# Three more row buffers for the expert gathers of the second layer's context mixer, paid for with half of the Gram buffer

## The chip, the cores and the metric

One core of a Trainium2 chip runs the whole program. The metric is the device time in microseconds (us), as the median of several executions.

## What is computed

The program is a two-layer block over 256 tokens and 256 context tokens (width 1024), followed by one hybrid layer. Only the first block touches the change. In each of its layers:

```
hc = modulate(xc, ...);  yc, ctx_states = token_mixer(hc, emit = not last)   # context
h  = modulate(x, ...);   y, _ = token_mixer(h, states = ctx_states)          # tokens
x  = x + gt1 * y
x  = x + gt2 * peer(modulate(x, ...))                                        # experts of the tokens
if not last: the same for xc
```

`token_mixer` holds a recurrence over tokens for 16 heads and two directions (`rwkv_scan`), here in chunks of 64 tokens. In the second layer the context mixer has `emit=False`: it only makes the states. `peer` picks for every token 8 x 16 experts out of 16384, and

```
u = take(peer_u, eidx);  act = gelu(einsum('td,thkd->thk', h, u)) * gw
v = take(peer_v, eidx);  out = einsum('thk,thkd->td', act, v)
```

so each token needs 128 rows of `peer_u` and 128 rows of `peer_v`, 4 KB each.

## The kernel before

**The job.** Since `peer` of one stream doesn't depend on the mixer that comes next, its work is spread through the stages of that mixer. `k.job` is the running job. It has 256 rows to take: row `r` is one indirect DMA (512 KB: for each of 128 tokens its expert's row of `peer_u`), issued by GpSimd in `gather_row`, and one VectorE instruction over 128 x 1024 in `use_rows` (L2092), which makes 128 dot products. When the first 128 rows are done, `weigh_tile` makes weights of them, and from then on values are open: a batch is four gathers of `peer_v` (`gather_part`, L2149), a small copy (`pick_weights`) and 8 matmuls of 512 columns (`use_batches`, L2118).

**Buffers and order.** Row gathers use the slots in `job.shared.slots`, four of them here, in turn (`job.turn % len(slots)`). Row `r` goes into the slot that row `r-4` had, so its gather waits until VectorE has used row `r-4`. Batches use eight other slots, four in the weight ring and four in `more`, so two batches are in the air. The program of every stage is written out ahead: VectorE's part says after which of its own steps it takes how many rows, TensorE's part when it takes a batch, and then `fetch_rows` writes GpSimd's part for the stage: all rows and batches that the stage uses and does not have yet, and the ones that fit in the slots after that. It sorts them by the step at which their slot came free. GpSimd works through this list in order, so a gather that waits holds up all behind it.

**The stage in question.** `rwkv` of the second layer's context mixer, with `k.job` the tokens' job of the first layer. `project_keys` comes first (18 weight blocks, 26 rows), then eight calls of `rwkv_unit` (four quarters of the heads, two directions). I call them units 0 to 7. A unit, with the names that the rows show:

1. VectorE makes `KR` (L911), takes 4 rows, makes `Ld`, `LdT`, `NT` (L923, L924) from TensorE's products (L962, L963), takes 1 row, makes `X` (L991).
2. `invert_pairs`: 12 steps in which TensorE multiplies (L724, L719) and ScalarE copies each product back (L700). VectorE isn't in this chain when a job runs; beside it, it takes 18 rows (14 when values are open) and makes `G` (L1002), the masked Gram products, after steps 4 and 5. After step 8 TensorE and ScalarE make the sigmoids of the next unit (L780, L781).
3. The recurrence: TensorE and ScalarE pass `R`, `W`, `S`, `state` to and fro (L1121 to L1154, L1044 to L1067), once for each of two chunks. Meanwhile VectorE makes the sums of the next unit (L790 to L801) and its rates (L823 to L825) and takes 3 rows. Between the two chunks ScalarE raises the sums to exponentials (L809, L811), from which VectorE makes `C` (L846).
4. All engines meet before the next unit's `KR`.

Units 0 to 3 run with values closed and take 26 rows each. Before unit 4 the tile is weighed; units 4 to 7 take 22 rows and, in all, about five batches each. The rest of the job is done in `finish_experts`, where eight row slots are in use and the matrix engine waits for the rows.

`G` has 128 columns per product, of which the mixer without `emit` uses 64. Its flat form also serves as `squares` in `project_keys`, ahead of the units.

Of the kernel before, what the change touches and what calls it, by code (L numbers as in the profile page):

```python
# [13 lines left out]
P = 128  # L14
# [22 lines left out]
class Core:  # L37


    def __init__(self, nc, ctx):  # L40
# [26 lines left out]
        self.spare_slots, self.own_slots, self.windows = [], False, []  # L67
# [1117 lines left out]
def project_keys(k, L, w, order, rhs, b, first, emit, then=None, mod=None):  # L1185
# [10 lines left out]
    squares = b.G[:].rearrange("p h i n t -> p (h i n t)").rearrange("p (j t) -> p j t", j=8)  # L1196
# [184 lines left out]
def rwkv(k, L, z, states, emit, w, rhs, order, o=None, spare=None, then=None, hosts=None, restore=(), mod=None):  # L1381
# [4 lines left out]
    with ExitStack() as mem:  # L1386
# [4 lines left out]
        with ExitStack() as inner:  # L1391
            u = buffers(k, inner, tot=[2, 2, 4], pc=[2, 2, 4], KR=[2, 2, 256], C=[2, 4, 2, 64], CT=[4, 2, P], G=[2, 2, 4, P], W=[4, 2, 2, 64],
# [11 lines left out]
            units[0].first = True  # L1404
            if hosts is None and k.job is not None:
                more = buffers(k, inner, more=[4, 1024]).more
                hosts = spare_rows(k, 8, *(more[:, j, :] for j in range(4)))
            project_keys(k, L, w, order, rhs, u, units[0], emit, None if emit else then, mod)
            enter_ring(k, hosts)
# [574 lines left out]
class Slot:  # L1984

    def __init__(self, rows, landed):
        self.rows, self.landed = rows, landed
        self.freed, self.taken, self.left, self.step = None, False, 0, 0  # L1990
# [8 lines left out]
    def leave(self, sem, value, step, order=0):  # L1999
        self.freed, self.taken, self.step, self.left = (sem, value), False, step, order  # L2000
# [10 lines left out]
class Experts:  # L2011
# [3 lines left out]
    def __init__(self, shared, lists, x, layer):  # L2015
        self.shared, self.lists, self.x, self.layer = shared, lists, x, layer
        self.row, self.fetched, self.places, self.turn, self.stage = 0, 0, {}, 0, 0
# [62 lines left out]
def use_rows(k, dve, n):  # L2080


    job = k.job
# [3 lines left out]
    for r in range(job.row, min(job.row + n, 2 * SLOTS)):  # L2087
        tile, slot = divmod(r, SLOTS)
        place = place_row(job, r)
# [38 lines left out]
def gather_row(k, pool, r):  # L2128

    job, b = k.job, k.job.shared  # L2130
    place = place_row(job, r)
# [42 lines left out]
def fetch_rows(k, pool):  # L2174
# [5 lines left out]
    rows = range(job.fetched, min(job.row + len(job.shared.slots), 2 * SLOTS))  # L2180
# [3 lines left out]
    wanted, picked = [(place_row(job, r).step, 2, r, 0) for r in rows], 0  # L2184
# [13 lines left out]
def enter_ring(k, more):  # L2198
# [296 lines left out]
def finish_experts(k, job, then=None):  # L2495
# [14 lines left out]
    with ExitStack() as inner:  # L2510
# [3 lines left out]
        b.slots, job.turn = [*own, *extra[0:4]], 4  # L2514
# [67 lines left out]
def choose_last(k, l, dram, x, mod, job, then):  # L2582
# [13 lines left out]
    with ExitStack() as mem:  # L2596
# [11 lines left out]
        b.slots, job.turn = [*own, *extra[8:12]], 0  # L2608
# [1301 lines left out]
```

## Time and profile before

| | us |
|---|---|
| median of 3 runs | 5279.18 |
| lowest, highest | 5279.08, 5311.7 |
| the profiled execution's own time | 5297.07 |
| its span, first to last instruction | 5295.1 |

Busy over the span: TensorE 3740.9 us (71%), VectorE 2454.9 (46%), GpSimd 1706.1 (32%), ScalarE 1087.5 (21%). These shares are means over stages with different limits, so the stage has to be read by itself: units 0 to 7 lie between 2170 and 2723 us of the span. The profiled execution is 17.9 us above the median; durations below come from it.

### The profile page before, as it was taken

How to read it: one execution, taken by the hardware profiler on the slowest of the kernel's cores; microseconds unless marked ns; L12 is line 12 of the kernel's file. 1: busy time of each engine (PE TensorE's matmuls, PEld its weight loads, DVE VectorE, ACT ScalarE, POOL GpSimd, SP SyncE). 2: the span in 40 equal slices, each digit the busy share in tenths (PEclk: the TensorE clock that was granted, in tenths of full speed). 3: DMA queues.
4: the chain of work that ended last, by engine and by line, in shares of the span. 5: the costliest groups of instructions: out<-in, count | busy, mean ns of one | idle time of the engine just before them, and what ended most of it. 6: DMA issues, size and time to landing. Idle time of an engine off the chain costs nothing. (4 is left out here: it accounts for less than half of the span.)

```text
span 5295.1 us, 87998 instructions
## 1 busy us (share of the span) xinstructions
PE 3740.9 (71%) x36238; PEld 2819.0 (53%) x36238; DVE 2454.9 (46%) x5650; ACT 1087.5 (21%) x2789; POOL 1706.1 (32%) x1745
## 2 busy tenths in 40 slices
PE   7989896976767886765645599988430325877788
PEld 6777684864545563654421187776300001766677
DVE  2756547675553264774450023663968240143310
ACT  1234311232222111342310022442100000111300
POOL 0000003245564244465566500000567776000000
PEclk9999997987787897886767799998765667888899
DMA  5423246777786587677789743003799999312242
GB/s 210 132 94 130 89 151 260 263 239 253 270 273 237 213 333 289 228 251 256 271 318 368 301 140 115 3 3 108 287 360 350 362 362 345 124 59 62 88 142 105
DMA packets 298909, 1117.72 MB, mean 211 GB/s; under 512 B 33681, under 2 KB 39073, under 8 KB 289953
## 3 DMA queue, kind: packets, MB, share of 16 engines
q0 software_dynamic: 221184, 805.40, 42.5%
q1 hardware_dynamic: 77344, 306.90, 16.9%
q8 instruction: 280, 4.59, 0.4%
q14 instruction: 101, 0.82, 0.0%
HBM read 1111.13 MB, written 1.05 MB: 210 GB/s over the span
## 5 line engine op out<-in xcount | busy, mean ns | idle before, releaser
L2135 POOL DMA_INDIRECT ring<-in_peer_u,expert_number x624 | 720.4, 1154 | 1204.8 <-DVE expert_number L2446 566.4
L2092 DVE CUSTOM_DVE_ANT_0 ring<-ring,tok 128x1024 f32<-128x1024 f32 x624 | 754.8, 1225 | 482.7 <-DMA ring<-in_peer_u,expert_number 454.8
L2118 PE MATMUL psum<-spare,picked 128*32 128x512 f32 x1472 | 283.2, 870 | 520.5 <-issue 241.5
L2118 PEld LDWEIGHTS psum<-spare,picked 128*32 128x32 f32 x1472 | 60.2, 138 | 737.0 <-issue 736.6
L2149 POOL DMA_INDIRECT spare<-in_peer_v,expert_turned x368 | 352.3, 957 | 157.1 <-issue 92.9
L177 PE MATMUL psum<-h,weight_ring 128*128 128x256 f32 x1728 | 386.0, 387 | 22.6 <-PEq L96 22.6
L177 PEld LDWEIGHTS psum<-h,weight_ring 128*128 128x128 f32 x1728 | 336.3, 195 | 71.7 <-issue 23.9
L1823 PE MATMUL psum<-h,weight_ring 128*128 128x256 f32 x1344 | 294.3, 380 | 3.5 <-PEq L96 3.5
L1823 PEld LDWEIGHTS psum<-h,weight_ring 128*128 128x128 f32 x1344 | 254.8, 190 | 41.7 <-issue 7.5
L1339 PE MATMUL psum<-h,weight_ring 128*128 128x256 f32 x1056 | 236.8, 386 | 8.6 <-PEq L96 8.6
L2149 POOL DMA_INDIRECT weight_ring<-in_peer_v,expert_turned x174 | 181.9, 1045 | 139.0 <-PE psum L2118 90.1
L1339 PEld LDWEIGHTS psum<-h,weight_ring 128*128 128x128 f32 x1056 | 203.3, 194 | 41.3 <-issue 12.7
L2291 DVE SCALAR_TENSOR_TENSOR x_tokens<-psum,gate,x_tokens 128x128 f32<-128x128 f32 x32 | 8.6, 343 | 438.7 <-PE psum L2280 438.7
L2092 DVE CUSTOM_DVE_ANT_0 spare<-spare,tok 128x1024 f32<-128x1024 f32 x144 | 176.0, 1225 | 32.1 <-DMA spare<-in_peer_u,expert_number 24.8
L2118 PE MATMUL psum<-weight_ring,picked 128*32 128x512 f32 x696 | 141.1, 789 | 64.4 <-POOL picked L2169 30.3
L700 ACT ACTIVATE E<-psum 128x256 f32<-128x256 f32 x240 | 90.1, 383 | 419.3 <-PE psum L724 378.0
L2135 POOL DMA_INDIRECT spare<-in_peer_u,expert_number x144 | 160.2, 1113 | 49.6 <-issue 41.3
L2149 POOL DMA_INDIRECT more<-in_peer_v,expert_turned x120 | 119.9, 999 | 138.9 <-PE psum L2118 75.9
L2826 POOL MEMSET picked<- 128x1512 f32 x1 | 1.4, 1358 | 485.5 <-POOLq L96 485.5
L724 PE MATMUL psum<-TT,E 64*64 64x64 f32 x3072 | 125.7, 226 | 43.2 <-ACT TT L700 19.2
L724 PEld LDWEIGHTS psum<-TT,E 64*64 64x64 f32 x3072 | 113.3, 139 | 64.3 <-ACT TT L700 21.4
L1672 DVE SCALAR_TENSOR_TENSOR zc<-u,vec,zc 128x256 f32<-128x256 f32 x336 | 134.7, 482 | 0.0
(617 smaller groups left out, 7368.3 us busy)
## 6 DMA issues: line engine op xcount, KB each, us to landing
weight_ring<-in_w_in SPq DMA_DIRECT2D x226, 512.0 KB
ring<-in_ada_w SPq DMA_DIRECT2D x24, 1024.0 KB, 12.0
weight_ring<-in_w_q SPq DMA_DIRECT2D x48, 512.0 KB
weight_ring<-in_ada_w SPq DMA_DIRECT2D x16, 1024.0 KB, 6.5
weight_ring<-in_w_out SPq DMA_DIRECT2D x32, 512.0 KB
gate_ring<-in_w_gate SPq DMA_DIRECT2D x32, 512.0 KB, 3.6
weight_ring<-in_w_mlp_in SPq DMA_DIRECT2D x32, 512.0 KB
weight_ring<-in_w_mlp_out SPq DMA_DIRECT2D x8, 2048.0 KB
```

Source lines behind the costliest of these rows:

```text
L177: mm = pe.matmul(k.bank(slot, tokens), ring[:, slot, j * P:j * P + P], rhs(j), start=(j == 0), stop=(j == w.kt - 1))
L700: act.activation(out[:, g], product(q, g), ACT.Copy).then_inc(k.act_step.up(), 1)
L724: mm = pe.matmul(product(q, g)[h, n, :], left[h, g, n, :], rhs, start=not onto, stop=True, skip_group_check=onto)
L1339: mm = pe.matmul(k.bank(4 + slot, 256), k.ring[:, slot, j * P:j * P + P], rhs(j), start=(j == 0), stop=(j == 7))
L1672: ins = dve.scalar_tensor_tensor(conv[:, j, :], src, scale, conv[:, j, :], ALU.mult, ALU.add)
L1823: mm = pe.matmul(k.bank(slot, 256), k.ring[:, slot, j * P:j * P + P], normed[:, j, :] if i >= blocks else rhs(j), start=(j == 0), stop=(j ...
L2092: dve.tensor_tensor_reduce(place.rows, place.rows, b.tok[:, tile, :], 1.0, 0.0, ALU.mult, ALU.add, b.dots[:, tile, slot:slot + 1]).then_in ...
L2118: mm = pe.matmul(out, place.window.columns[:, strip, first:first + STRIP], part.rows[:, 512 * half:512 * half + 512], start=(m % BATCHES = ...
L2135: pool.indirect_dma_start(place.rows, None, b.tables["u"], bass.IndirectOffsetOnAxis(ap=b.number[:, r:r + 1], axis=0)).then_inc(place.sem, 16)
L2149: pool.indirect_dma_start(part.rows, None, b.tables["v"], bass.IndirectOffsetOnAxis(ap=job.lists.turned[:, token:token + 1], axis=0)).then ...
L2291: dve.scalar_tensor_tensor(part, k.psum[:, P * j:P * j + P], job.lists.gate[:, j:j + 1], part, ALU.mult, ALU.add).then_inc(k.vec_step.up(), 1)
L2826: pool.memset(lent.picked[:], 0.0).then_inc(k.pool_step.up(), 1)
```

## The change

- In the mixer without `emit` and with a job running, `G` gets 64 columns per product instead of 128 (4 KB per partition given up).
- `more` grows from four rows to seven. The first four serve the batches as before. The other three are row slots, in `k.more_rows`, from the first unit to the end of the last; two of them serve as `squares` before that.
- A row no longer takes the slots in turn. It takes the slot that has been free longest, out of the shared ones and `k.more_rows`. `fetch_rows` gathers ahead as long as a slot is free: seven rows instead of four in the units.
- In the last unit `k.more_rows` is emptied before GpSimd's list is written, so four rows are ahead at its end, as before.

No instruction is added or taken away, other than waits on slots.

```diff
-        G=[2, 2, 4, P]
+        G=[2, 2, 4, P if emit or k.job is None else 64]
...
+            row_hosts = []
+            u.squares = u.G[:]... if emit or k.job is None else None
             if hosts is None and k.job is not None:
-                more = buffers(k, inner, more=[4, 1024]).more
+                more = buffers(k, inner, more=[7, 1024]).more
                 hosts = spare_rows(k, 8, *(more[:, j, :] for j in range(4)))
+                row_hosts = spare_rows(k, 12, *(more[:, j, :] for j in range(4, 7)))
+                u.squares = more[:, 4:6, :]...
             project_keys(k, L, w, order, rhs, u, units[0], emit, None if emit else then, mod)
-            enter_ring(k, hosts)
+            enter_ring(k, hosts, row_hosts)
...
     def leave(self, sem, value, step, order=0):
-        self.freed, self.taken, self.step, self.left = (sem, value), False, step, order
+        self.freed, self.taken, self.step, self.left, self.since = (sem, value), False, step, order, next(Slot.uses)
...
+def row_slots(k, r):
+    slots = [*k.job.shared.slots, *k.more_rows]
+    return [slot for slot in slots if not slot.taken]
+
-def place_row(job, r):
+def place_row(k, r):
+    job = k.job
     if r not in job.places:
-        slots = job.shared.slots
-        job.places[r] = slots[job.turn % len(slots)].take()
-        job.turn += 1
+        job.places[r] = min(row_slots(k, r), key=lambda slot: slot.since).take()
...
-    rows = range(job.fetched, min(job.row + len(job.shared.slots), 2 * SLOTS))
+    rows = range(job.fetched, job.row)
+    while len(rows) + job.fetched < 2 * SLOTS and row_slots(k, job.fetched + len(rows)):
+        rows = range(job.fetched, job.fetched + len(rows) + 1)
+        place_row(k, rows[-1])
...
-        k.spare_slots = [*k.job.shared.weight_ring, *more]
+        k.spare_slots, k.more_rows = [*k.job.shared.weight_ring, *more], rows
...
-        k.spare_slots = []
+        k.spare_slots, k.more_rows = [], []
```

## Rows read from the trace of the kernel before

**Rows 1.** Busy time by stage: units 0, 3 and 6, then a stretch of `finish_experts`

```profile
core 0: us, PE busy (x) PEld busy (x) DVE busy (x) ACT busy (x) POOL busy (x), PEclk, DMA share, GB/s
2170.50:2227.50 57.00, 40.50 (x720) 34.23 (x721) 43.25 (x77) 21.61 (x61) 33.43 (x28) 0.77 0.73 242
...
2337.80:2392.40 54.60, 37.50 (x688) 31.49 (x688) 43.33 (x77) 20.82 (x59) 34.85 (x27) 0.84 0.77 251
...
2568.98:2647.84 78.86, 53.60 (x800) 38.99 (x800) 38.63 (x70) 22.08 (x61) 46.94 (x47) 0.78 0.80 278
...
2738.00:2766.00 28.00, 0.00 (x0) 0.00 (x0) 24.62 (x40) 0.00 (x0) 21.91 (x21) 0.50 0.99 377
```

**Rows 2.** Waits of VectorE, units 0 to 3 (us in total, times, longest)

```profile
DVE ring L2092 <- DMA ring<-in_peer_u,expert_number: 42.2, 54, 2.0
```

**Rows 3.** VectorE in order of time: unit 0, then `finish_experts` (start, us)

```profile
2174.33 1.22 DVE L2092 CUSTOM_DVE_ANT_0 ring<-ring,tok 128x1024 f32<-128x1024 f32 x1 [0.80 <-DMA ring<-in_peer_u,expert_number]
2177.24 1.22 DVE L2092 CUSTOM_DVE_ANT_0 ring<-ring,tok 128x1024 f32<-128x1024 f32 x1 [1.68 <-DMA ring<-in_peer_u,expert_number]
...
2180.88 1.23 DVE L2092 CUSTOM_DVE_ANT_0 ring<-ring,tok 128x1024 f32<-128x1024 f32 x1 [0.41 <-DMA ring<-in_peer_u,expert_number]
...
2196.47 1.23 DVE L2092 CUSTOM_DVE_ANT_0 ring<-ring,tok 128x1024 f32<-128x1024 f32 x1 [0.67 <-DMA ring<-in_peer_u,expert_number]
...
2205.05 1.22 DVE L2092 CUSTOM_DVE_ANT_0 ring<-ring,tok 128x1024 f32<-128x1024 f32 x1 [0.85 <-DMA ring<-in_peer_u,expert_number]
...
2738.04 1.23 DVE L2092 CUSTOM_DVE_ANT_0 ring<-ring,tok 128x1024 f32<-128x1024 f32 x1
...
2770.39 1.23 DVE L2092 CUSTOM_DVE_ANT_0 spare<-spare,tok 128x1024 f32<-128x1024 f32 x1 [0.57 <-DMA spare<-in_peer_u,expert_number]
```

**Rows 4.** ScalarE in order of time, ends of units 0 to 3

```profile
2218.23 0.63 ACT L809 ACTIVATE E<-E 128x512 f32<-128x512 f32 x1 [0.47 <-DVE E L796]
...
2273.06 0.63 ACT L809 ACTIVATE E<-E 128x512 f32<-128x512 f32 x1 [3.00 <-DVE E L801]
...
2328.54 0.63 ACT L809 ACTIVATE E<-E 128x512 f32<-128x512 f32 x1 [4.26 <-DVE E L796]
...
2377.64 1.28 ACT L809 ACT_TABLE_LOAD   x1
2383.61 0.63 ACT L809 ACTIVATE E<-E 128x512 f32<-128x512 f32 x1 [4.69 <-DVE E L801]
...
2387.72 0.94 ACT L1067 ACTIVATE state<-psum,pc 128x64 f32<-128x64 f32 x4 [0.77 <-PE psum L1154]
```

**Rows 5.** VectorE in order of time, end of unit 3

```profile
2391.62 0.69 DVE L846 TENSOR_TENSOR C<-X,E 64x512 f32<-64x512 f32 x1
```

**Rows 6.** GpSimd and TensorE in order of time, unit 1

```profile
2263.39 1.12 POOL L2135 DMA_INDIRECT ring<-in_peer_u,expert_number  x1 [0.30 <-issue]
...
2266.09 1.27 PE L1154 MATMUL psum<-W,CT 128*64 128x64 f32 x16 [0.88 <-issue]
...
2268.40 0.69 PE L1121 MATMUL psum<-S,KR 64*64 64x64 f32 x8 [1.04 <-issue]
```

**Rows 7.** TensorE (busy, clock, DMA share, GB/s) by stretches, units 1 and 6

```profile
2240.00:2258.00 18.00, 14.53 (x326) 1.00 0.85 282
...
2572.00:2575.00 3.00, 2.81 (x65) 1.00 0.93 317
...
2578.00:2581.00 3.00, 1.83 (x10) 0.50 0.97 365
2581.00:2584.00 3.00, 1.17 (x6) 0.50 1.01 392
```

**Rows 8.** TensorE in order of time, unit 5, under 8 gathers

```profile
2524.08 1.12 PE L724 MATMUL psum<-constants,X 64*64 64x64 f32 x16 [3.74 <-issue]
2528.42 1.12 PE L724 MATMUL psum<-X,NT 64*64 64x64 f32 x16 [3.23 <-issue]
```

**Rows 9.** Waits of VectorE from 2400 to 2715 us, units 4 to 7

```profile
DVE ring L2092 <- DMA ring<-in_peer_u,expert_number: 114.3, 38, 9.9
```

More of the change, by code:

```diff
@@ L1 @@
+import itertools
 import math
@@ L1195, in project_keys @@
     kz = z[:, 8:16, :]
-    squares = b.G[:].rearrange("p h i n t -> p (h i n t)").rearrange("p (j t) -> p j t", j=8)
+    squares = b.squares
     norm = b.TT[0:16].rearrange("p i n t -> p (i n t)")[:, 0:256]
@@ L1391, in rwkv @@
         with ExitStack() as inner:
[L1392 removed]
+            u = buffers(k, inner, tot=[2, 2, 4], pc=[2, 2, 4], KR=[2, 2, 256], C=[2, 4, 2, 64], CT=[4, 2, P], G=[2, 2, 4, P if emit or k.job is None else 64], W=[4, 2, 2, 64],
                         R=[2, 2, 64], S=[2, 2, 64], LdT=[2, 4, 64], NT=[2, 4, 64], Ld=[2, 4, 64], E1=[2, 4, 64], E2=[2, 4, 64],
@@ L1404, in rwkv @@
             units[0].first = True
+            row_hosts = []
+            u.squares = u.G[:].rearrange("p h i n t -> p (h i n t)").rearrange("p (j t) -> p j t", j=8) if emit or k.job is None else None
             if hosts is None and k.job is not None:
-                more = buffers(k, inner, more=[4, 1024]).more
+                more = buffers(k, inner, more=[7, 1024]).more
                 hosts = spare_rows(k, 8, *(more[:, j, :] for j in range(4)))
+                row_hosts = spare_rows(k, 12, *(more[:, j, :] for j in range(4, 7)))
+                u.squares = more[:, 4:6, :].rearrange("p n c -> p (n c)").rearrange("p (j t) -> p j t", j=8)
             project_keys(k, L, w, order, rhs, u, units[0], emit, None if emit else then, mod)
-            enter_ring(k, hosts)
+            enter_ring(k, hosts, row_hosts)
             for n, operands in enumerate(units):
@@ L1984 @@
 class Slot:
+    uses = itertools.count(1)
     def __init__(self, rows, landed):
         self.rows, self.landed = rows, landed
-        self.freed, self.taken, self.left, self.step = None, False, 0, 0
+        self.freed, self.taken, self.left, self.step, self.since = None, False, 0, 0, 0
     def take(self):
@@ L2016, in __init__ @@
         self.shared, self.lists, self.x, self.layer = shared, lists, x, layer
-        self.row, self.fetched, self.places, self.turn, self.stage = 0, 0, {}, 0, 0
+        self.row, self.fetched, self.places, self.stage = 0, 0, {}, 0
         self.batch, self.batches_fetched, self.groups = 0, 0, {}
@@ L2183, in fetch_rows @@
     batches = range(first, max(last, min(last + ahead, job.open_batches())))
-    wanted, picked = [(place_row(job, r).step, 2, r, 0) for r in rows], 0
+    wanted, picked = [(place_row(k, r).step, 2, r, 0) for r in rows], 0
     for m in batches:
@@ L2195, in fetch_rows, with enter_ring @@
             gather_row(k, pool, n)
-def enter_ring(k, more):
+def enter_ring(k, more, rows):
     if k.job is not None:
-        k.spare_slots = [*k.job.shared.weight_ring, *more]
+        k.spare_slots, k.more_rows = [*k.job.shared.weight_ring, *more], rows
 def leave_slots(k, pe):
@@ L2513, in finish_experts @@
         extra = spare_rows(k, 8, *(spare.spare[:, j, :] for j in range(20)))
-        b.slots, job.turn = [*own, *extra[0:4]], 4
+        b.slots = [*own, *extra[0:4]]
         k.spare_slots, k.own_slots, k.windows = extra[4:20], True, [Window(spare.picked[:, n]) for n in range(6)]
@@ L2607, in choose_last @@
         own, windows, marks = b.slots, k.windows, {}
-        b.slots, job.turn = [*own, *extra[8:12]], 0
+        b.slots = [*own, *extra[8:12]]
         k.spare_slots, k.own_slots, k.windows = [*extra[12:16], *extra[0:8], *b.weight_ring], True, [Window(lent.picked[:, n]) for n in range(6)]
```

6 lines of the change are left out of this document (3 added, 3 removed).

## The prediction

> **What bounds the kernel now.** The page of the whole span can't decide this: VectorE is busy for 46% of it, and the change acts on 8 of its stages. I read first the busy time of each stage, then the waits of VectorE in the stages with the new slots, then the order of time at the end of a unit, to see whether a wait of VectorE delays anything.
>
> In units 0 and 3 VectorE is busy for 43.3 of 57.0 and 54.6 us, TensorE for 40.5 and 37.5 [rows 1]; units 1 and 2, 54.9 and 55.4 us long, repeat the pattern. VectorE waits there for one thing that matters: a row that has not landed, 42.2 us in 54 waits over the four units [rows 2], some 10.5 in each. So 43.3 of work, 10.5 of waits and under 1 us of meeting the others fill the unit: VectorE has no other idle time, and it is the engine that ends it. The reader should see this at the end of unit 3 too. ScalarE has loaded its table by 2378.9 us and then waits 4.69 us for VectorE's sums [rows 4]. `C` ends at 2392.3 [rows 5], after `state` at 2388.7 [rows 4]. Both say that TensorE and ScalarE were ready earlier.
>
> Why do rows come late? In the long stretch beside the inversion four rows take from 2196.47 to 2205.05, 2.15 us each, with a wait for the landing before nearly every one [rows 3]. VectorE alone would do one in 1.15 us, the step from one row to the next where none is late. With four slots one row costs a quarter of the loop "use, gather, land, use". In `finish_experts`, with eight slots, 23 steps from 2738.04 to 2770.39 take 32.35 us, 1.41 us each [rows 3], and there the DMA engines are at a share of 0.99 with 377 GB/s [rows 1]. So with four slots the loop sets the pace, and with eight the DMA engines do.
>
> **The change part by part.**
>
> *Narrower `G`, moved `squares`.* The same instructions on the same counts of elements, in other places. The squares lie in two of the new rows, which hold no row before the first unit. I take 0; no row bounds a difference in placement, and I allow 1 us either way for the 32 writes of `G` in the eight units together.
>
> *Slots by longest free instead of in turn.* With one ring of slots that all go through the same hands this is the same order. Where slots are added (the finishing stages) the fresh ones come first, as before. In the last choice of experts the fresh ones now come ahead of the old ones, and none of these has anything to wait for. 0 us.
>
> *Seven slots in units 0 to 3.* The first three gathers of unit 0 need no used slot. From then on row `r` waits for `r-7`. A unit needs 26 rows: at 1.41 us each that is 36.7 us of supply against 43.3 us of VectorE's own work, so the supply is enough on the mean. Within the unit the hard stretch is 18 rows beside the inversion, 18 x 1.15 + 2 x 0.67 for `G` = 22 us, against 18 x 1.41 = 25.4 us less what is ahead. Seven slots hold up to 9.9 us of supply, of which some 5 rows are there when the stretch begins (5 rows were taken just before it). That covers the 3.4 us that are missing. I leave 1 us of waits per unit, 4 in all, and remove 38 of the 42 us from VectorE.
>
> *What is late next.* With its waits gone VectorE is no longer last. From the order of time: the exponentials could start earlier by the wait that ScalarE shows, 0.47, 3.00, 4.26 and 4.69 us in units 0 to 3 [rows 4], together 12.4 us. `state` then ends 3.65 us ahead of where `C` ended (2392.31 less 2388.66 in unit 3 [rows 4, 5]; the same difference in the other three), 14.6 us over four units. In unit 0, the two waits ahead of `Ld`, 0.80 and 1.68 us, and 0.41 us after it delay the inversion itself [rows 3]; they add 2.9 us. The sum is 29.9 us: that is how much the chain of TensorE and ScalarE lets go, 7.5 us per unit. It is below the 38 us, so it is the bound, and 30 us is the most these four units can give unless that chain also gets faster.
>
> *What more gathers in a row do to that chain.* This is the dispute of the case. Below four gathers without a pause in unit 1, from 2263.39 on, TensorE starts two groups late, with nothing to release it, 0.88 and 1.04 us [rows 6], and the products that ScalarE waits for come late with them; 1.9 us over 4 gathers, 0.5 us each. In unit 6, below 13 gathers without a pause, TensorE drops from 65 matmuls in 3 us to 10 and 6, its granted clock from 1.00 to 0.50 (2.4 to 1.2 GHz), with the DMA share from 0.93 to 0.97 and 1.01 [rows 7]. In unit 5, below 8 gathers, it stands for 3.74 and 3.23 us [rows 8], 0.9 us per gather. In units 0 to 3 the share is 0.73 to 0.77 on the mean [rows 1], because the four-slot loop breaks the stream up. Seven slots remove these breaks: the 18 rows beside the inversion become one stream at about the pace of `finish_experts`, where the share is 0.99. The lower bound of the extra loss is 0 (GpSimd's pace of 1.41 us with VectorE busy is not the 1.25 us of the batches, so the queue need not grow). The upper bound is 18 x 0.9 = 16.2 us per unit, less the 2.5 us or so that the chain already loses today in its short streams, 13.7 us. I take 0.4 us a gather, near the row of unit 1, since that one has rows only and VectorE at work, as here: 7.2 - 2.5 = 4.7 us. Of the 7.5 us per unit 2.8 remain, 11 us for the four.
>
> On this the Trainium skill speaks in "Runtime: NRT & Kernel Launch", section Instruction fetch mechanics: an engine's sequencer fetches the next block of instructions by a queue of its own while the present one runs, and a long program's cost for it is mostly hidden. If nothing but that stood behind the starts without a releaser, they should not grow with the gathers, and the sum would be that of the first rival. The drop from 65 matmuls to 6 doesn't agree with "hidden", whatever its mechanism; the trace doesn't name one.
>
> *Seven slots in units 4 to 7.* VectorE waits 114.3 us for rows [rows 9], which looks like the larger prize. It isn't: unit 6 is 78.9 us long with 53.6 us of TensorE [rows 1], VectorE's 14 rows beside the inversion are not in its chain, and the stalls of TensorE's own issue set the pace. GpSimd's list keeps its order, only with rows 3 further on: behind each batch's wait VectorE runs 3 rows (3.4 us) further before it stands. Nobody reads `C` before the unit ends. Where a late row does delay TensorE (unit 5, ahead of `Ld` and `X`), unit 6 shows what comes instead, the trickle under the 13 gathers. On the other hand up to seven rows instead of four can follow a batch without a pause, a stream of 11 instead of 8. I take 0, with -10 (unit 5 gains) and +8 us (three more gathers in each of 2 streams per unit at 0.3 us) as ends.
>
> *Sum.* -11 + 0 + 0. The profiled execution would go from 5297.1 to 5286, and the median from 5279.2 to 5268.
>
> **The rivals.**
>
> *The chain lets go of all of it.* The extra loss is near 0. For it: at a share of 0.85 in unit 1 TensorE does 326 matmuls in 18 us at full clock [rows 7], and the total of bytes is unchanged. Against it: the later stretches [rows 7, 8]. It gives -29.9 + 4 = -26, 5253 us. The page's rule leads here too.
>
> *The stream starves TensorE: slower than before.* In the 26 us of the inversion the loss is 0.7 to 0.9 us for each of 18 gathers, as in unit 5. At 0.8 it is 14.4 - 2.5 = 11.9 us a unit; the chain's 7.5 us are used up and 4.4 us are added, four times: +18, 5297 us. It decides from an extra loss of 7.5 us per unit on, that is 0.56 us per gather. For it: the stalls of unit 5, and the halved clock in unit 6 [rows 7, 8]. Against it: VectorE's rows set a slower pace than batches, and unit 1 lost less [rows 6].
>
> *The change doesn't do what it says.* If the gathers' landing slows with more of them under way, seven slots give the same pace per row. The 1.41 us against 2.15 speak against that [rows 3]. 5279 us, within 3.
>
> *The late rows of units 4 to 7 were in the chain.* If unit 5's waits ahead of `Ld` and `X` go and the trickle moves into other gaps, another 10 us or so go on top of the first rival: 5243 us.
>
> **How the numbers follow.** Partial gain, -4 to -20 around -11: 0.38. All of it: 0.28. Slower, +5 to +50 around +18: 0.23. Nothing: 0.06. More than all: 0.05. The likeliest gives 5268. From 5243 to 5296 I leave out about half of the slower case's tail and the far end of the last, 2 in 10. A measurement of this kernel can tell a change of about 1%, 53 us, from none. Faster by more would need more than both row waits' bounds together; I give it 0.04. Slower by more needs the upper bound of 13.7 us in every unit and a loss in units 4 to 7: 0.05. Within 1%: 0.91.
>
> **What would show the steps right or wrong.** In the changed kernel's profile, units 0 to 3: the waits of VectorE for rows fall from 42 us to under 8, else the supply step is wrong. ScalarE's wait for the sums (L809) is gone. Where VectorE waits instead, it is for ScalarE's exponentials ahead of `C`, or at the meeting for `state`. TensorE's starts without a releaser tell the rest: a unit of 48 us with few of them is the first rival, 52 us the forecast, over 56 us the second. In units 4 to 7 the waits for rows fall by 10 to 20 us and the lengths don't change. The prediction would be wrong if the granted clock of TensorE rises or falls throughout the units, as the chain's 30 us come from rows at the clocks of today.

## The result: slower, and the profile after

In 20 runs of each, the changed kernel took 5314.25 us (median; 5285.82 to 5329.47) and the kernel before 5293.62 us; the ratio is 1.0034, 95% interval 1.0023 to 1.0045. The effect is a third of a per cent, but clear of the noise. Of the forecast's own 5279.18 us that ratio makes 5297.1 us, 1 us above the top of the range (the ratio of the two medians, 1.0039, makes 5299.8). Another 14 us of the distance to 5314 are in the median of the kernel before, which I had from three runs.

The profiled execution took 5317.47 us with a span of 5315.4, against 5297.07 and 5295.1 before. A unit begins when VectorE starts `KR`; from one start to the next (us):

| unit | 0 | 1 | 2 | 3 | 4 | 5 | 6 | all |
|---|---|---|---|---|---|---|---|---|
| before | 57.0 | 54.8 | 55.5 | 58.2 | 94.3 | 78.7 | 78.9 | 477.3 |
| after | 62.1 | 62.8 | 51.3 | 53.9 | 99.3 | 82.1 | 88.4 | 499.9 |

(Unit 3's figure holds the weighing behind it.) The seven units lose 22.6 us: 4.7 in units 0 to 3 and 17.9 in units 4 to 6. The rest of the program gives 2 us back.

The busy time by stage of the kernel after, units 0, 4 and 6, with the columns of [rows 1]:

```profile
2171.07:2233.17 62.10, 44.66 (x720) 36.08 (x721) 43.33 (x78) 22.04 (x61) 36.90 (x31) 0.78 0.74 262
2401.24:2500.51 99.27, 60.88 (x800) 41.52 (x800) 38.32 (x70) 22.23 (x61) 48.93 (x53) 0.70 0.68 239
2582.57:2670.96 88.39, 58.46 (x800) 39.48 (x800) 38.24 (x70) 22.17 (x61) 47.04 (x48) 0.73 0.70 250
```

VectorE's work is the same 43.3 and 38 us as in [rows 1]. So it waits more, though not for rows. TensorE does the same matmuls but is busy with them for longer: 44.7 against 40.5 us in unit 0, 58.5 against 53.6 in unit 6. Over units 0 to 3 its granted clock is 0.78 after and 0.81 before, over units 4 to 6 0.74 and 0.76. Its waits of the kernel after, units 0 to 3 (us in total, times, longest), answer to [rows 2]:

```profile
DVE E L791 <- ACT NT L782: 24.4, 2, 15.0
DVE ring L2105 <- DMA ring<-in_peer_u,expert_number: 12.5, 13, 2.3
DVE C L847 <- ACT E L812: 7.0, 3, 2.9
DVE more L2105 <- DMA more<-in_peer_u,expert_number: 3.3, 6, 1.0
```

The row waits fell from 42.2 to 15.8 us, as the change meant them to. In their place stands a wait for the sigmoids (L782), which ScalarE makes at the end of the inversion: the chain of TensorE and ScalarE has become late. ScalarE's own waits in the same stretch say where:

```profile
ACT E L701 <- remote: 21.5, 5, 7.1
ACT TT L701 <- remote: 14.7, 3, 6.8
ACT X L701 <- remote: 6.5, 2, 3.3
```

L701 is the copy of a product out of PSUM, inside the inversion. "Remote" means that the semaphore was raised, but 1.5 us or more after the end of any instruction that raises it, so that the profile names none. Over units 0 to 3 these waits are 42.7 us in ten, against 2.6 before. The mark has two flaws: it leaves out delays under 1.5 us, and it counts the time in which TensorE was still at work on the product. A measure without them is the **lateness** of a copy: from the end of its product (or from when ScalarE is free, if that is later) to its start. Summed over the 96 copies of the inversion in units 0 to 3 it is 66.6 us after and 27.6 before; in units 4 to 6 (72 copies) 69.5 and 57.0. It is computed from the two traces; ends of matmuls are modelled in them. Unit 1 shows what lies under it. The columns are those of [rows 1], kernel after:

```profile
2254.00:2257.00 3.00, 1.12 (x16) 0.93 (x16) 2.55 (x6) 0.38 (x1) 2.39 (x3) 0.50 1.05 358
...
2260.00:2263.00 3.00, 0.00 (x0) 0.00 (x0) 2.98 (x5) 0.00 (x0) 2.11 (x3) 0.50 1.02 410
...
2266.00:2269.00 3.00, 0.00 (x0) 0.00 (x0) 0.87 (x2) 0.00 (x0) 2.33 (x3) 0.50 1.03 418
...
2272.00:2275.00 3.00, 3.00 (x62) 3.00 (x61) 0.00 (x0) 1.15 (x3) 0.00 (x0) 0.50 0.29 119
```

The same stretch in order of time (start, us):

```profile
2255.12 1.12 PE L725 MATMUL psum<-constants,X 64*64 64x64 f32 x16 [2.47 <-ACT X L701]
...
2257.60 0.38 ACT L701 ACTIVATE TT<-psum 128x256 f32<-128x256 f32 x1 [2.54 <-PE psum L725]
...
2258.04 1.12 PE L725 MATMUL psum<-X,NT 64*64 64x64 f32 x16 [1.80 <-issue]
...
2264.04 0.38 ACT L701 ACTIVATE TT<-psum 128x256 f32<-128x256 f32 x1 [6.05 <-remote]
2264.28 0.94 POOL L2148 DMA_INDIRECT ring<-in_peer_u,expert_number  x1 [0.30 <-issue]
...
2264.47 1.12 PE L725 MATMUL psum<-X,NT 64*64 64x64 f32 x16 [5.32 <-issue]
2265.52 0.94 POOL L2148 DMA_INDIRECT more<-in_peer_u,expert_number  x1 [0.30 <-issue]
...
2271.18 0.66 ACT L701 ACTIVATE E<-psum 128x256 f32<-128x256 f32 x2 [6.75 <-remote]
```

The copy at 2264.04 takes the product that TensorE made from 2255.12 to 2256.24, and TensorE starts at 2264.47, when that copy is through. So the time goes between the product's end and the copy's start, 7.8 us here. The trace has the semaphore raised at 2264.01, and ScalarE starts 0.03 us later: the signal is late, not ScalarE. Whether the last matmul itself ended late, the modelled ends can't tell. GpSimd sends a gather every 1.28 us meanwhile on the mean, and VectorE does a row every 1.25 us from 2258.18 to 2265.64. At 2272 the DMA share falls to 0.29, and TensorE does 62 matmuls in 3 us. Then rows are all ready, and VectorE waits for the chain. The engines have the same instructions to do; they now stand in a row instead of side by side.

The stretch of units 4 to 7, VectorE's waits of the kernel after, answers to [rows 9]:

```profile
DVE ring L2105 <- DMA ring<-in_peer_u,expert_number: 52.7, 12, 11.6
DVE E L791 <- ACT NT L782: 48.0, 3, 17.7
...
DVE more L2105 <- DMA more<-in_peer_u,expert_number: 9.5, 2, 8.5
```

### The profile page after: what moved, and what is told of

Same layout as the page of the kernel before. It is cut to its first block and busy times, and to the rows that moved or that the text cites. A ratio compares the mean times of both kernels' runs of the same rounds, so it can differ in the third digit from the quotient of the medians.

```text
span 5315.4 us, 87997 instructions
## 1 busy us (share of the span) xinstructions
PE 3762.9 (71%) x36238; PEld 2819.6 (53%) x36238; DVE 2450.7 (46%) x5650; ACT 1088.4 (20%) x2789; POOL 1710.8 (32%) x1745
## 5 line engine op out<-in xcount | busy, mean ns | idle before, releaser
L2148 POOL DMA_INDIRECT ring<-in_peer_u,expert_number x543 | 626.8, 1154 | 1086.4 <-DVE expert_number L2462 566.4
L2105 DVE CUSTOM_DVE_ANT_0 ring<-ring,tok 128x1024 f32<-128x1024 f32 x543 | 656.6, 1224 | 312.9 <-DMA ring<-in_peer_u,expert_number 276.0
L178 PE MATMUL psum<-h,weight_ring 128*128 128x256 f32 x1728 | 386.3, 388 | 22.6 <-PEq L97 22.6
L2162 POOL DMA_INDIRECT spare<-in_peer_v,expert_turned x368 | 350.2, 952 | 147.5 <-issue 94.3
L701 ACT ACTIVATE E<-psum 128x256 f32<-128x256 f32 x240 | 89.7, 383 | 440.7 <-PE psum L725 312.1
L725 PE MATMUL psum<-TT,E 64*64 64x64 f32 x3072 | 137.5, 233 | 49.8 <-issue 29.4
```

Of the source, the lines that this page charges most:

```text
L178: mm = pe.matmul(k.bank(slot, tokens), ring[:, slot, j * P:j * P + P], rhs(j), start=(j == 0), stop=(j == w.kt - 1))
L701: act.activation(out[:, g], product(q, g), ACT.Copy).then_inc(k.act_step.up(), 1)
L725: mm = pe.matmul(product(q, g)[h, n, :], left[h, g, n, :], rhs, start=not onto, stop=True, skip_group_check=onto)
L2105: dve.tensor_tensor_reduce(place.rows, place.rows, b.tok[:, tile, :], 1.0, 0.0, ALU.mult, ALU.add, b.dots[:, tile, slot:slot + 1]).then_in ...
L2148: pool.indirect_dma_start(place.rows, None, b.tables["u"], bass.IndirectOffsetOnAxis(ap=b.number[:, r:r + 1], axis=0)).then_inc(place.sem, 16)
L2162: pool.indirect_dma_start(part.rows, None, b.tables["v"], bass.IndirectOffsetOnAxis(ap=job.lists.turned[:, token:token + 1], axis=0)).then ...
```

## The experiments

The runs fell to chips of two kinds, told apart by the kernel before on the same chip: **kind A**, where it takes 5292 to 5317 us (the result above belongs here), and **kind B**, where it takes 5107 to 5112 us. I had not looked for this, and it turned out to matter more than any slot. Besides the result, kind A was met on two chips, one of them twice, and kind B on two; "kind" stands for whatever differed between them. All ratios are to the kernel before on the same chip. "Remote" is the sum of ScalarE's waits marked so, "late" the sum of the lateness of the inversion's copies, each in units 0 to 3, then in units 4 to 6. The last three columns come from one profiled execution, which isn't always a typical one: slots5b's took 25 us less than the median of its run, inflight4's 14 us less, slots6b's 9 us more. Of the kernel before there is no profile on kind B; slots4, with the same instructions, stands in for it.

| kernel | kind | ratio, 95% interval | units 0 to 3, 4 to 6 (us) | remote (us) | late (us) |
|---|---|---|---|---|---|
| before | A | 1 | 225, 252 | 2.6, 55.6 | 28, 57 |
| changed, 7 slots (after) | A | 1.0034 (1.0023 to 1.0045) | 230, 270 | 42.7, 85.8 | 67, 70 |
| changed again (after7) | A | 1.0054 (1.0035 to 1.0072) | 249, 279 | 54.5, 95.0 | 82, 74 |
| changed again (after7c) | A | 1.0046 (1.0025 to 1.0066) | 244, 277 | 44.8, 99.0 | 63, 68 |
| 4 slots (slots4) | B | 1.0007 (0.9993 to 1.0021) | 227, 229 | 0, 0 | 4, 3 |
| 5 slots (slots5) | B | 0.9901 (0.9879 to 0.9924) | 208, 204 | 0, 0 | 4, 3 |
| 5 slots (slots5b) | A | 1.0039 (1.0024 to 1.0055) | 219, 273 | 16.5, 89.5 | 45, 77 |
| 6 slots (slots6) | B | 0.9875 (0.9853 to 0.9897) | 203, 191 | 0, 0 | 4, 3 |
| 6 slots (slots6b) | A | 1.0071 (1.0055 to 1.0087) | 241, 282 | 38.8, 94.1 | 62, 71 |
| 7 slots, at most 3 on their way (inflight3) | B | 1.0081 (1.0056 to 1.0106) | 231, 280 | 0, 0 | 4, 3 |
| 7 slots, at most 4 (inflight4) | A | 0.9972 (0.9953 to 0.9990) | 218, 247 | 15.0, 23.4 | 51, 42 |
| the same (inflight4b_2) | B | 0.9942 (0.9924 to 0.9960) | 203, 235 | 0, 0 | 4, 3 |
| 7 slots, at most 5 (inflight5) | A | 1.0050 (1.0031 to 1.0069) | 236, 279 | 33.5, 82.8 | 62, 64 |
| 4 slots, at most 4 (slots4_inflight4) | A | 0.9984 (0.9964 to 1.0005) | 224, 249 | 0, 21.4 | 31, 39 |
| half of each row, 6 slots (halfbytes) | A | 1.0060 (1.0041 to 1.0078) | 229, 278 | 31.7, 87.1 | 65, 72 |
| 1/16 of each row, 6 slots (tiny64_2) | B | 0.9860 (0.9836 to 0.9885) | 196, 194 | 0, 0 | 4, 3 |
| memsets for row gathers (nodma_2) | B | 0.9726 (0.9701 to 0.9750) | 178, 163 | 0, 0 | 4, 3 |
| the same (nodma_3) | A | 0.9725 (0.9686 to 0.9764) | 178, 177 | 0, 2.8 | 4, 19 |
| paced gathers, 7 slots (paced_2) | B | 0.9927 (0.9906 to 0.9948) | 205, 228 | 0, 0 | 4, 3 |
| the same (paced_3) | A | 0.9952 (0.9931 to 0.9972) | 214, 245 | 4.6, 13.6 | 46, 48 |

Where do the two kinds part? The kernel before on kind A and slots4 on kind B have the same instructions. Taken step by step, kind A is 1 us behind at 1240 us of slots4's span, 54 at 1750, 56 at 2340, 108 at 2870, 106 at 3570, 172 at 4330 and 174 at the end. So 171 of the 174 us arise in three stretches, all with gathers of values on their way, and the rest of the program, units 0 to 3 with four slots included, takes the same time on both, within 4 us a stretch.

### The layout alone, and the number of slots

slots4 keeps the narrower `G`, the moved squares and the new choice of slots, without the row slots; slots5 and slots6 have one and two of the three.

```
-                row_hosts = spare_rows(k, 12, *(more[:, j, :] for j in range(4, 7)))
+                row_hosts = []           # slots5: range(4, 5); slots6: range(4, 6)
```

> The changed kernel with its layout (G of 64 columns, the squares and seven row buffers in one tile, the choice of the buffer free longest) but with no row slot among them: rows have the four ring slots as before. Theory A (the deeper stream of gathers starves TensorE and ScalarE): the layout costs nothing, ratio to the kernel before 0.998 to 1.002, units 0 to 3 within 1 us of 57.0, 54.9, 55.4 and 58.1 us. Rival B (the layout or the order itself costs, for instance G or the squares at another address): ratio 1.003 to 1.0045, as with the whole change.

> As the changed kernel, but with one row slot more in place of three (five in all). Theory A: the loss comes with the number of gathers on their way, so one more row takes part of VectorE's row waits away (42 us in units 0 to 3 fall to some 30) with few stalls of the TensorE to ScalarE hand-over; ratio 0.998 to 1.001. Rival C (any row ahead costs as much as it gains, evenly): ratio 1.001, a third of the loss of the whole change. Both leave fewer than 10 us of ScalarE waits marked remote in units 0 to 3, against 42.7 us with seven slots.

> As the changed kernel, but with two row slots more (six in all). Theory A: a threshold between four and seven, so the ratio lies between 0.999 and 1.003 and ScalarE waits marked remote in units 0 to 3 between 10 and 35 us. Rival C (evenly): 1.002.

On kind B the layout costs nothing that can be told: 1.0007 (unit 3, at 59.5 us, is 1.4 us over what was expected). On kind A it was not timed alone; the nearest run there, four slots with a limit of four on the gathers, has 0.9984, which makes it unlikely that the loss lies in the layout. Five and six slots gained 1 and 1.25%, far beyond what either theory allowed, and there was not one remote wait. Units 0 and 5 of four slots, then of six, both on kind B:

```profile
2112.47:2169.20 56.73, 37.27 (x721) 31.58 (x721) 43.21 (x77) 22.20 (x61) 34.79 (x28) 0.83 0.76 243
2420.52:2494.88 74.36, 48.47 (x768) 33.09 (x768) 38.63 (x70) 21.00 (x59) 49.97 (x48) 0.77 0.85 298
```

```profile
2113.78:2165.65 51.87, 38.32 (x721) 32.65 (x721) 43.22 (x78) 22.16 (x61) 38.96 (x30) 0.80 0.85 291
2383.68:2445.02 61.34, 44.92 (x768) 30.02 (x768) 38.56 (x69) 20.96 (x59) 48.46 (x48) 0.86 0.97 359
```

Unit 5 has a DMA share of 0.97 and TensorE at a granted clock of 0.86; the same share meant starvation in [rows 7]. So a share near 1 doesn't starve TensorE by itself. Theory A, in which the full DMA engines did it, fell with this, and the kernels had to run beside the changed one on one chip.

> The changed kernel itself, unaltered, timed beside the kernel before on one chip. In the runs with four to six slots neither TensorE issue stalls nor ScalarE waits marked remote came up, though the gathers kept the DMA share at 0.85 to 1.0, and the kernel before took 5112 us, not 5294. Theory A (as first put: deep queues of gathers starve TensorE wherever the DMA share is near 1; seven slots cross a threshold that six do not): ratio 1.003 and some 40 us of remote waits in units 0 to 3, on any chip. Theory F (starvation belongs to the chip that the result was measured on, not to the number of slots): where the kernel before takes some 5112 us, ratio 0.985 to 0.990 and no remote waits; where it takes some 5290 us, ratio 1.003 with remote waits.

> Six slots again, on one chip with seven. Theory A: at least 1% faster than seven slots and without remote waits. Theory F: within 0.4% of seven slots on whichever chip; if the kernel before takes some 5290 us, remote waits of 20 us or more in units 0 to 3 here too and a ratio between 0.999 and 1.004.

> Five slots again, on one chip with seven. Theory A: ratio 0.990, as before. Theory F: 0.990 where the kernel before takes some 5112 us; where it takes some 5290 us a ratio of 0.997 to 1.003, with fewer remote waits than with seven slots.

> The changed kernel once more, as the yardstick on whichever chip this is. Theory F (the outcome goes with the chip): where the kernel before takes some 5110 us, ratio 0.983 to 0.990, no remote waits, units 0 to 3 of 49 to 53 us and units 4 to 6 of 61 to 67; where it takes 5290 to 5320 us, ratio 1.003 to 1.006 with over 40 us of ScalarE's remote waits in units 0 to 3. Theory A (seven slots starve TensorE on any chip): over 1.003 in both.

These fell to kind A, and theory F holds: the same six-slot kernel that gains 1.25% on one kind loses 0.7% on the other, with 38.8 us of remote waits in place of none. Its sizes were missed, though: 1.0071 where up to 1.004 was expected for six slots, 1.0039 where up to 1.003 was for five. On kind A even one slot more costs 0.4%; in its profile, of an execution faster than most, units 0 to 3 are shorter (219 us) and units 4 to 6 longer (273). Seven slots unchanged never fell to kind B. That they gain there is likely from six slots, and from seven with a brake (0.9942 and 0.9927, below), but not measured.

### Fewer gathers on their way

GpSimd waits, ahead of each gather of the mixer, for the landing of the third (fourth, fifth) one before it.

```
+def wait_in_flight(k, pool, sem, landed):
+    if k.more_rows:
+        if len(k.on_way) >= 4:
+            pool.wait_ge(*k.on_way[-4])
+        k.on_way.append((sem, landed))
```

> The changed kernel with its seven row slots, but GpSimd issues a gather in this mixer only once the third gather before it has landed: at most three gathers of 512 KB are on their way at a time. Theory A (what hurts is the depth of the queue of gathers, not the rows held ready): ScalarE waits marked remote in units 0 to 3 fall from 42.7 us to under 8, the stage takes no longer than before, ratio 0.996 to 1.001. Rival D (what hurts is VectorE running its row products closer together, or the seven buffers being read and written): the stalls stay, ratio 1.003. Rival E (GpSimd, held by its waits, is late with gathers and weights of units 4 to 7): row waits come back and units 4 to 7 take longer than 94, 79 and 79 us, ratio above 1.003 with few remote waits.

> Seven slots, but a gather is issued only once the fourth one before it has landed (with three the stage became longer: GpSimd was held, ratio 1.0081). Theory A and F agree where TensorE starves: remote waits in units 0 to 3 fall from 42.7 us to under 15 and the ratio is below that of seven slots. Where TensorE doesn't starve, the limit only costs: ratio 0.4% to 1% above that of seven slots. Rival E (waits on GpSimd hold gathers and weights back whatever the chip): row waits in units 4 to 7 well above those of seven slots.

> Seven slots with at most five gathers on their way. On a chip that starves: remote waits of units 0 to 3 between those of the limit of four (15.0 us) and of no limit (54.5 us), some 30, and a ratio between 0.997 and 1.005. On one that doesn't: closer to the changed kernel than a limit of three (1.008) by far, within 0.4% of it.

> Four row slots as before the change, with the limit of four gathers on their way (rows and value parts together). Theory G (the limit's gain of 0.28% on the chip that starves came from the values of units 4 to 7, whose gathers the kernel before also sends without limit: 55.6 us of ScalarE's remote waits there): on such a chip remote waits in units 4 to 6 fall from 55.6 to under 30 us, ratio 0.997 to 1.000. Theory H (the gain came from rows held ready, once their stream is kept shallow): ratio 1.000 to 1.003 with units 0 to 3 at 55 to 58 us each. On a chip that doesn't starve both give 1.000 to 1.005: GpSimd is held and nothing comes back.

> Seven slots with at most four gathers on their way once more, beside the paced kernel on one chip: 0.997 again on a chip that starves; the paced kernel is within 0.3% of it if pace is all that the limit of four gave. On a chip that doesn't starve, 0.990 to 1.003.

A limit of three was too tight (it fell to kind B, where nothing is to be cured): VectorE met the late end of GpSimd's list. At the end of unit 4 all other engines are through by 2423.6 us and GpSimd by 2443.1. VectorE's waits in units 4 to 7 of that kernel:

```profile
DVE KR L912 <- PEq L97: 64.2, 4, 22.0
DVE more L2105 <- DMA more<-in_peer_u,expert_number: 33.0, 16, 8.6
```

A limit of four is faster than both kernels on kind A, 0.9972, and faster than the one before on kind B, 0.9942, where it costs 0.7% against six free slots. A limit of five does nearly nothing (33.5 us remote, lateness 62). With four slots the limit brings the remote waits of units 4 to 6 from 55.6 to 21.4 us but the units only from 252 to 249 us: the interval holds 1, and theory G's ratio is met without being shown. Theory H's ratio, 1.000 to 1.003, is not met. Seven slots with the limit have 218 and 247 us, four slots with it 224 and 249. That is a difference of 8 us, taken on two chips, and one of the two executions lies 14 us under its median: in which units the rows held ready pay is not shown. Of my expectation that remote waits end below 15 us, 15.0 is the edge.

### Bytes, GpSimd's work, or pace

The row gathers bring 512 (64) of 1024 columns from as many places:

```
+    wide = 512 if k.more_rows else 1024
+    pool.indirect_dma_start(place.rows[:, 0:wide], None, b.tables["u"].rearrange("n (t c) -> (n t) c", c=wide), ...
```

> Six row slots, and each row gather of this mixer brings 512 of the 1024 columns (2 KB from each of 128 places instead of 4 KB; VectorE multiplies all 1024 by zero, so the row sums and the expert weights that follow from them are left out). GpSimd's instructions, their number, the packets' number per gather (as far as one packet is one row) and all waits stay. Theory I (bytes in flight starve the engines): on a chip that starves, remote waits of units 0 to 3 fall from 38.8 us (six slots) to under 10. Theory J (the number of gathers or GpSimd's work for them, whatever their bytes): they stay above 25 us. Row waits of VectorE vanish under both, units 0 to 3 take 46 to 50 us where nothing starves.

> As the run with half of each row, but each row gather of this mixer brings 64 of the 1024 columns (256 bytes from each of 128 places), six row slots. The row sums are multiplied by zero, so the expert weights are left out. Theory J (GpSimd's back-to-back gathers starve the hand-overs by their number and the work of describing them, whatever the bytes: half the bytes left 31.7 us of remote waits against 38.8): on a chip that starves, remote waits of units 0 to 3 stay above 20 us. Theory K (the time in which DMA engines are at work, which half the bytes still left at a share of 0.46): they fall below 5 us.

Units 0 to 3 on kind A with half rows, then with whole rows (slots6b). These windows, and those of units 0 to 3 below, end ahead of the weighing. The DMA share is 0.46 and 0.69:

```profile
2178.29:2404.47 226.18, 167.82 (x2816) 137.63 (x2816) 170.95 (x308) 86.13 (x240) 144.19 (x108) 0.79 0.46 129
```

```profile
2177.58:2415.57 237.99, 170.84 (x2816) 141.85 (x2816) 172.46 (x308) 85.86 (x241) 135.96 (x108) 0.76 0.69 236
```

The remote waits stay: 31.7 against 38.8 us, and 87.1 against 94.1. The lateness in units 0 to 3 stays too, 65 against 62 us, in more and shorter delays: the longest are 2.6 us in place of 6.8, and they come at a DMA share of 0.61 to 0.69. Hence it is not bytes, nor full DMA engines: theory I falls, J stands. A sixteenth of the bytes fell to kind B, where it could only show that six slots are near the floor (0.9860 against 0.9875); theory K is untested. That VectorE's row waits vanish with half the bytes was wrong: 13.1 us are left of 14.1 on kind A, and 18.3 of 21.4 with a sixteenth on kind B. So bytes don't set the pace of rows here either.

Then a memset of the row buffer in place of each row gather (rows are zero; their products are left out), and, apart from it, gathers with a pause:

```
+        pool.memset(place.rows, 0.0).then_inc(place.sem, 1)        # nodma
```

```
+def pause(k, pool):                                                # paced, behind every gather
+    if k.more_rows:
+        pool.wait_ge(k.paused.sem, k.paused.count)
+        pool.memset(k.idle, 0.0).then_inc(k.paused.up(), 1)        # 128x256
```

> Each row gather of this mixer's units is replaced by a GpSimd memset of the same row buffer (about 0.96 us by the 128x1024 memset elsewhere in the trace, against 0.94 for a gather), so GpSimd is as busy but describes no transfer; the rows are zero, their products left out. Value gathers stay. Theory J: remote waits and TensorE issue stalls of units 0 to 3 vanish (under 3 us) and the units take 44 to 50 us. Rival L (GpSimd's business itself, or VectorE's row products closer together, starves the others): remote waits stay above 20 us.

> The memsets in place of the row gathers once more; on the chip that doesn't starve they gave 0.9726, with no remote waits to begin with. On a chip that starves, theory J: no remote waits or TensorE issue stalls in units 0 to 3 (under 3 us), units of 44 to 51 us. Rival L (GpSimd's business itself): remote waits above 20 us there.

> Seven row slots, no limit on the gathers on their way, but behind each gather of this mixer GpSimd fills 256 columns of a buffer that nobody reads, some 0.35 us, so that gathers follow each other at 1.6 us and not 1.24. Theory J: on a chip that starves, remote waits of units 0 to 3 fall from some 45 to 55 us to under 15, with as many gathers in flight as seven slots allow; ratio 0.995 to 0.999. Theory A (depth of the queue): the waits stay above 30 us and the ratio at 1.003 to 1.006. On a chip that doesn't starve: 0.985 to 0.995.

> The paced gathers once more; on the chip that doesn't starve they gave 0.9927 (a limit of four gathers 0.9942, six slots at full pace 0.9875). On a chip that starves, theory J: remote waits of units 0 to 3 under 15 us and a ratio of 0.994 to 0.999. Theory A (depth of the queue of gathers): remote waits above 30 us, ratio 1.002 to 1.006.

Units 0 to 3, then units 4 to 6, with memsets for the row gathers on kind A:

```profile
2169.46:2344.37 174.91, 140.06 (x2816) 119.92 (x2816) 167.63 (x308) 86.95 (x241) 103.88 (x109) 0.89 0.03 8
2347.37:2523.90 176.53, 137.43 (x2368) 96.25 (x2368) 115.35 (x208) 64.76 (x181) 139.81 (x145) 0.90 0.59 189
```

Units 0 to 3 take 45.6, 43.1, 43.1 and 46.1 us on kind A and 45.9, 43.1, 43.1 and 46.2 on kind B. That is just below the 44 us expected at the least. Without the row gathers the two kinds are one in these units, with a lateness of 4 us on both. GpSimd, busy for 59% of them against 57 to 61% with the gathers, and VectorE's rows at their closest harm nobody: rival L falls. In units 4 to 6, where gathers of values stay, kind A takes 177 us and kind B 163, with a lateness of 19 and 3. What differs between the kinds in these stages is what a gather does to the others.

The paced kernel keeps seven slots. On kind A its remote waits are 4.6 us in units 0 to 3 and 13.6 in units 4 to 6. At 0.9952 it has the lowest ratio there of those that compute all, though its interval and that of the limit of four overlap:

```profile
2163.69:2374.68 210.99, 158.82 (x2816) 133.12 (x2816) 171.97 (x308) 86.44 (x241) 168.53 (x216) 0.81 0.80 273
```

So gathers some 0.35 us further apart starve less than gathers back to back at 1.24 us, though seven may be under way. But the remote waits flatter the pause: the lateness in units 0 to 3 is 46 us, a quarter to four tenths less than the 62 to 82 of six and seven slots, and the limit of four leaves 51. What both do away with is the long delays: the longest are 3.5 and 3.3 us in place of 5 to 9. Pace and number on their way aren't wholly apart in it: slower gathers also queue up less.

## Why the prediction was wrong

**What bounds the kernel.** VectorE's row waits did end the units, and they fell. But the 29.9 us that the chain of TensorE and ScalarE "lets go" were read from a kernel in which that chain was already disturbed. With four slots ScalarE waits 38.0 us for the sums in units 0 to 3 on kind B and 12.4 on kind A: the chain on kind A was already slower, under the cover of VectorE's waits. Its lateness was 27.6 us over units 0 to 3, against 4.3 on kind B. That is 5.8 us a unit, where the prediction put the loss of its short streams at 2.5.

**Layout and choice of slots.** Taken as 0; measured 1.0007 on kind B, with 1 inside the interval. Right there, and not measured alone on kind A.

**Seven slots in units 0 to 3.** Row waits below 8 us were forecast, 15.8 came. The wait of ScalarE for the sums did go, as said. VectorE waits for the exponentials ahead of `C`, as named, for 7.0 us, but for 24.4 us for the sigmoids at the end of the inversion, which was not named. The supply of 1.41 us a row was taken from a stretch with the DMA engines full; the runs with fewer bytes show that the units' pace doesn't come from there.

**What more gathers in a row do to that chain.** This step failed by its size, and with the next one it makes the miss. The extra loss was put at 4.7 us a unit. The lateness of the copies grew by 39.0 us over units 0 to 3, 9.8 us a unit (13.5 in after7, 8.8 in after7c). I had taken 0.4 us a gather, from unit 1 [rows 6], against 0.9 from unit 5 [rows 8]. An estimate of the same price from the lengths: units 0 to 3 got 4.7 us longer instead of 29.9 shorter, 34.6 us or 8.7 a unit; with the 2.5 us taken as already lost that is 11.2 us over 18 gathers, 0.62 us each. In after7 the four units are 23 us longer, and the same sum gives 0.87. The second rival was to decide from 0.56 on, and it did. I had chosen the row nearest in kind (rows only, VectorE at work), but its stream was four gathers long, and the loss grows along the stream. Counted over units 0 to 3, by the place that the latest gather has in its stream (gathers less than 0.6 us apart) when the product is ready:

| mean lateness of a copy (us) | no gather | gathers 1 to 8 | 9 to 16 | 17 and on |
|---|---|---|---|---|
| kernel before, kind A | 0.02 | 0.29 | none | none |
| seven slots, three profiles, kind A | 0.03 | 0.35 | 1.21 | 2.64 |
| six slots, kind B | none | 0.05 | 0.04 | 0.03 |

The kernel before has no stream of over 8 gathers in these units, so its rows held only the low price. A short stream's price can't be carried to a long one. The mark set for the second rival, units over 56 us, was passed by units 0 and 1, while units 2 and 3 at 51.3 and 53.9 lie near the forecast's 52. Three profiles of the one kernel give 230, 249 and 244 us; likely a few long stalls more or less decide.

**Seven slots in units 4 to 7.** The second step that failed, and most of the loss: taken as 0 with +8 as an end, it was +17.9 us in three of them. The prediction had seen that longer streams would follow a batch, and priced them at 0.3 us a gather. Row waits fell by 52 us, not 10 to 20, and VectorE's wait for the sigmoids came in their place (48.0 us). That VectorE's rows are not in TensorE's chain was true of kind A only: on kind B the three units went from 229 to 191 us with six slots. There rows were what bound them.

**The rivals.** The second rival's +18 us is the result (0.34% of 5294), but by luck: it had all of it in units 0 to 3, which lost 4.7 us. The first rival's -26 us for units 0 to 3 is what kind B showed with six slots, -24 (227 to 203). The last rival, late rows of units 4 to 7 in the chain, had a chance of 0.05 and is what kind B showed there, with -39 us and not some -10. So the mechanism of the second rival is that of kind A, and those of the first and the last are those of kind B, where the forecast gain would have been too small; I gave the first, right on kind B, a higher chance (0.28) than the second (0.23), and the partial gain, right on neither, the highest. The rival by which more slots don't quicken the rows held on neither: row waits fell on both. The trace of before had the warning, ScalarE's waits in units 4 to 6, and I took them as belonging to batches:

```profile
ACT TT L700 <- remote: 24.4, 8, 4.0
ACT E L700 <- remote: 14.1, 1, 14.1
ACT X L700 <- remote: 12.1, 3, 5.4
```

The condition on the clock, that it neither rises nor falls throughout, was nearly kept: 0.81 to 0.78 and 0.76 to 0.74.

On the Trainium skill's page "Runtime: NRT & Kernel Launch", section Instruction fetch mechanics, by which fetching is mostly hidden: on kind B no wait contradicts it. On kind A the sequencers do stand with nothing to wait for, even inside one product, whose matmuls carry no wait between them (kernel after, unit 5):

```profile
2522.63 0.36 PE L725 MATMUL psum<-E,E 64*64 64x64 f32 x5 [0.41 <-issue]
...
2523.36 0.38 PE L725 MATMUL psum<-E,E 64*64 64x64 f32 x4 [0.37 <-issue]
2524.10 0.21 PE L725 MATMUL psum<-E,E 64*64 64x64 f32 x1 [0.37 <-issue]
```

But from 2254 to 2272 us, with both of ScalarE's long waits, the trace has a single transfer of instructions, at 2255; no block of instructions lands at the end of either wait. Fetching is thus not shown as the cause.

**Open**: why the kinds differ; whether GpSimd's description of a gather or its 128 separate reads disturb the others (memsets remove both, half the bytes neither); and by which way a gather delays TensorE's signal to ScalarE. One rival stands untested, that recording takes part in it. The traces of kind A hold 31.9 to 34.2 thousand semaphore updates and those of kind B 40.9 to 44.0 thousand, of programs alike to within a few per cent, so on kind A records are missing, those of landings above all. Every timed execution has a recorded span and clock, and no run here shows the kernels without recording. Missing records also make some "issue" marks doubtful, as that of 5.32 us at 2264.47, where TensorE had just got its copy.

## What to carry to other kernels

More buffers for a stream of gathers buy run-ahead and, with it, long unbroken bursts; where bursts disturb another engine's chain, the waits removed on one engine come back on it, and a brake (a limit on gathers under way, or a short pause between them) can be worth more than another buffer. That was so on kind A; on kind B each brake cost more than it gave, against six slots. A cost that grows along a burst has to be priced from a burst as long as the one that the change makes. And a change of under a per cent should be timed on more than one chip: here the same edit, two more slots, was worth -1.25% and +0.7%.

## What the runs showed of the hardware

- Two kinds of chip run the kernel before in some 5110 and 5300 us. On kind B no copy of the inversion in units 0 to 6 starts more than 0.12 us late, in any of the eight profiles; on kind A, under streams of gathers, up to 9 us.
- Starvation doesn't go with bytes: half of them, at a DMA share of 0.46, left four fifths of the remote waits and all of the lateness.
- Gathers reach the same rate whether TensorE stands or works: 410 to 418 GB/s at a share of 1.02 to 1.03 on kind A with TensorE standing, and 421 on kind B (slots6) with TensorE busy for 2.98 of 3 us at the full clock:

```profile
2402.00:2405.00 3.00, 2.98 (x64) 1.72 (x58) 0.94 (x2) 1.15 (x3) 2.60 (x2) 1.00 1.04 421
```

- Without row gathers, units 0 to 3 agree on both kinds within 0.3 us each; the kernel before loses 171 of the 174 us between the kinds in stretches with gathers of values.
